# Projections, attentions, norms and gated sums of each block in one stage with a fixed order of steps

## The reference, cut to what matters

```
first block:  h = norm(x);  proj = h @ w_in -> xr, gr | dq, dk, dv | sq, sk, sv | gl
  o_lru  = gated linear recurrence(xr, gr)
  o_diff = 4 heads: softmax(norm(q0) norm(k0)^T + bias) - lam * softmax(norm(q1) norm(k1)^T + bias), causal, @ v
           then rms_norm over the head's 128 channels (sub-norm)
  o_swa  = 8 heads, 2 kv heads, window 128, with a sink logit per head
  merged = sum_n sigmoid(gl_n) * (o_n @ w_branch_n);   x += g * (merged @ w_out);  then a mixture of 32 experts
second block: h = norm(x);  proj = h @ w_in_2
  o_a = delta rule, both directions;  3 groups of 8 heads: window attention with dilation 1, 4, 16 (q, k normed)
  o_b = sum of the three groups, weighted by softmax of their log denominators
  mixed = sigmoid(gate_a) * (o_a @ w_dn_out) + sigmoid(gate_b) * (o_b @ w_attn_out);  x += mixed @ w_o;  then a gated FFN
```

## Time and profile before

| | us |
|---|---|
| median of 3 runs | 3631.92 (3628.58 to 3642.89) |
| the profiled execution | 3635.47 |
| its span, first to last instruction | 3633.5 |
| mean granted TensorE clock | 0.898 of full |

### The profile page before, as it was taken

How to read it: one execution, slowest core, us unless ns; L and a number is a source line. 1 busy time by engine, 2 the same in 40 slices (tenths; PEclk the granted TensorE clock), 3 DMA queues, 4 the chain that set the end, 5 groups by cost and what they waited for, 6 DMA issues and landing times. The chain is left out here.

```text
span 3633.5 us, 45934 instructions
## 1 busy us (share of the span) xinstructions
PE 3077.8 (85%) x18366; PEld 2419.9 (67%) x18366; DVE 2236.9 (62%) x2035; ACT 1594.3 (44%) x1712; POOL 250.9 (7%) x149
## 2 busy tenths in 40 slices
PE   7676669976899999999999909787868778979999
PEld 3554447764787788788878707686647665767777
DVE  6555643334798999999999744465545543336643
ACT  6523232221676777777777624222232331233322
POOL 0000000002011111111111000341000000000000
PEclk9886779995999999999999959898879777989999
DMA  7320102222899999999999741000202111223322
GB/s 310 99 71 18 47 1 93 93 97 111 308 370 370 367 373 376 372 373 372 376 370 379 272 149 63 14 4 26 75 13 70 47 35 47 93 59 93 93 81 81
DMA packets 207264, 604.81 MB, mean 166 GB/s; under 512 B 11426, under 2 KB 108706, under 8 KB 170500
## 3 DMA queue, kind: packets, MB, share of 16 engines
q1 hardware_dynamic: 197744, 568.52, 42.6%
q0 software_dynamic: 9216, 33.56, 2.5%
q10 hardware_dynamic: 148, 0.53, 0.0%
HBM read 581.57 MB, written 21.01 MB: 166 GB/s over the span
## 5 line engine op out<-in xcount | busy, mean ns | idle before, releaser
L1743 DVE TENSOR_TENSOR weight_ring_part<-weight_ring,weight_ring_part 128x2048 fp32r<-128x2048 f32 x384 | 860.5, 2284 | 103.0 <-ACT weight_ring_part L1684 102.9
L1684 ACT ACTIVATE weight_ring_part<-weight_ring 128x2048 fp32r<-128x2048 f32 x384 | 720.1, 1914 | 254.9 <-PE ps L192 132.6
L192 PE MATMUL ps<-weight_ring_part 128*128 128x512 f32 (+1 forms) x1328 | 527.6, 397 | 0.0
L287 DVE TENSOR_TENSOR weight_ring_part<-weight_ring,weight_ring_part 128x2048 fp32r<-128x2048 f32 x135 | 307.9, 2282 | 289.9 <-ACT weight_ring_part L284 288.2
L284 ACT ACTIVATE weight_ring_part<-weight_ring 128x2048 fp32r<-128x2048 f32 x135 | 256.8, 1903 | 369.8 <-PE ps L192 147.6
L190 PE MATMUL ps<-weight_ring_part,gathered_hi 128*128 128x512 f32 x1024 | 409.6, 400 | 1.8 <-DVE gathered_lo L1752 1.8
L192 PE MATMUL ps<-weight_ring_part,gathered_hi 128*128 128x512 f32 x1024 | 406.0, 396 | 0.0
L191 PE MATMUL ps<-weight_ring_part,gathered_lo 128*128 128x512 f32 x1024 | 405.9, 396 | 0.0
L190 PE MATMUL ps<-h1T_hi,weight_ring_part 128*128 128x512 f32 (+1 forms) x776 | 317.8, 409 | 54.3 <-PEq L339 29.3
L191 PE MATMUL ps<-h1T_hi,weight_ring_part 128*128 128x512 f32 (+1 forms) x776 | 307.9, 397 | 0.0
L192 PEld LDWEIGHTS ps<-weight_ring_part 128*128 128x128 f32 (+1 forms) x1328 | 253.3, 191 | 57.1 <-issue 0.8
(11 more groups left out here) (450 smaller groups left out, 4774.5 us busy)
## 6 DMA issues: line engine op xcount, KB each, us to landing
weight_ring<-in_w SPq DMA_DIRECT2D x190, 2048.0 KB, 9.1
weight_ring<-in_w_in SPq DMA_DIRECT2D x58, 1024.0 KB, 5.3
weight_ring<-in_w_ada SPq DMA_DIRECT2D x24, 1024.0 KB, 14.5
weight_ring<-in_w_ffn_up SPq DMA_DIRECT2D x44, 512.0 KB, 5.1
weight_ring<-in_w_ffn_down SPq DMA_DIRECT2D x11, 1024.0 KB, 4.9
chosen_rows<-y_rows SPq DMA_DIRECT2D x4, 2048.0 KB, 13.4
weight_ring<-in_w_branch SPq DMA_DIRECT2D x6, 1024.0 KB, 5.1
x_tok<-in_x SPq DMA_DIRECT2D x2, 2048.0 KB, 13.8
```

The costliest lines, as they stand in the source:

```text
L192: return nc.tensor.matmul(out, x[0], y[1], start=False, stop=stop)
L287: self.nc.vector.tensor_tensor(lo, full, hi, ALU.subtract).then_inc(self.split, 1)
L1684: nc.scalar.activation(hi_half(h), full_half(h), ACT.Copy).then_inc(w_rounded, 1)
L1743: nc.vector.tensor_tensor(lo_half(h), full_half(h), hi_half(h), ALU.subtract).then_inc(w_split, 1)
```

## The change: what it does

For each block, `project`, `attention`, the small stages and `merge_branches` are replaced by one stage, `stream`. A planner, `lay_out`, sets the order. It walks a list of **elements** (one element: 128 output channels; q, k, v, gate 8 k-steps, branch 4) and puts every other step at a place counted in k-steps; all engines then walk this one list, each doing its own part of every step.

The first block has 19 projection elements and 48 elements of gated sums, 440 k-steps; the second 36 and 32, 480 k-steps. The 24 attention units of each block start at k-steps 58 to 205 in the first and 58 to 306 in the second, 6, 5 or at least 8 k-steps apart. The gated sums' first element stands at k-step 152 and 288.

```diff
+def lay_out(elements, batches, units, gap, sources=(), subs=(), lse_from=None):
+    ...
+    for u in range(len(last_of) + 1):
+        put(last_of[u - 2] + 0.5 if u >= 2 else 0, "round", u)
+    for e, x in enumerate(elements):
+        put(ends[e], "out", e)
+        if x["kind"] == "v":
+            put(ends[e] + 2.5, "turn_v", e)
+    for b, batch in enumerate(batches):
+        done = ends[batch["elements"][-1]]
+        put(done + 2, "sums", b)
+        for j in range(len(batch["keys"])):
+            put(done + 5 + 2 * j, "spread", b, j)
+        spread_done[b] = done + 6 + 2 * len(batch["keys"])
+    for i, u in enumerate(units):
+        asked.append(max(asked[-1] + gap[i] if asked else 0, spread_done[u["batch"]]))
+    turned_at = [(min(asked[i + 2], asked[i] + 12) if i + 2 < N else asked[i] + 12) - 0.2 for i in range(N)]
+    for i in range(N):
+        put(asked[i], "scores", i)
+        put(min(asked[i + 1] + 0.3, asked[i] + 5) if i + 1 < N else asked[i] + 5, "norm", i)
+        put(turned_at[i], "turn", i)
+        put(turned_at[i] + 2, "weigh", i)
+        read_at.append(min(turned_at[i] + 5, turned_at[i + 1] + 0.1) if i + 1 < N else turned_at[i] + 5)
+        put(read_at[i], "read", i)
+    for h, i in enumerate(subs):
+        put(read_at[i] + 0.5, "sub_sums", h)
+        put(read_at[i] + 4, "sub_spread", h)
+    ...
+# PE: products of element e go to bank e % 2, which ACT alone empties
+if k0 == 0 and e >= 2:
+    copied(pe, e - 2)
+# PE: sums of squares, 4 matmuls of 128x2 per q or k element, instead of head_sum over 512 columns
+last = nc.tensor.matmul(ps[:, 2, at:at + 2], sq[:, slot_of_square(e), ...], head_sum[:, 0:P:HD], start=True, stop=True)
+# ACT: root of a batch of 4 elements (32 columns)
+nc.scalar.activation(root(b)[:, 0:m], ps[:, 2, 0:m], ACT.Sqrt, scale=1.0 / HD, bias=col("eps")).then_inc(rooted, 1)
+# DVE: reciprocal of 32 columns; for keys the factor is written out wide, PE transposes it, DVE multiplies
+nc.vector.reciprocal(factor(b)[:, 0:m], root(b)[:, 0:m])
+nc.vector.tensor_tensor(dst, dst, ps[:, 2, :], ALU.mult).then_inc(keys_scaled, 1)
+# DVE: the query's factor and the bias come with the scores, one instruction per segment
+for c, m, _, _, q_at, bias in u["scores"]:
+    last = nc.vector.scalar_tensor_tensor(s_row[:, c:c + m], scores[:, c:c + m], factor(u["batch"])[:, q_at:q_at + 1],
+                                          bias, ALU.mult, ALU.add)
+# ACT: gates by tanh (the table of the exponentials); branch copied out of PSUM
+nc.scalar.activation(merge["gate"][:, gate_at[e] % 2, :], bank, ACT.Tanh, scale=0.5)
+nc.scalar.activation(merge["branch"][:, branch_at[e] % 4, :], bank, ACT.Copy, scale=0.5)
-nc.vector.reciprocal(rinv, rinv)                      # 128x512, once per q or k element
-nc.tensor.matmul(ps[:, 4 + m % 2, :], head_sum, act_scratch[:, m % 2, :], start=True, stop=True)
+# second block: its input is stored once, since its room is used now, and loaded again in project_out
+sp.dma_start(x_mid.rearrange("(t p) d -> p t d", p=P), x_tok[:, :, :]).then_inc(x_stored, 16)
 sp.dma_start(w_ab, w_in2[:, 2048:2080].rearrange("(k p) n -> p k n", p=P)).then_inc(ab_loaded, 16)
 sp.dma_start(masks[:, :, :], a["joins"].rearrange("p (m i) -> p m i", i=HD)).then_inc(ab_loaded, 16)
```

More of the change, by code:

```diff
@@ L352, in build @@
         mix_at = len(ring.units)
-        for j in range(6):
-            ring.add_pair(wide(w_in, 512 * j), DK, 512, by_rows=(j == 4))
+        for j in range(2):
+            ring.add_pair(wide(w_in, 512 * j), DK, 512, by_rows=False)
+        for half in range(2):
+            for j in (4, 2, 3):
+                ring.add(wide(w_in, 512 * j)[:, :, 256 * half:256 * half + 256], DK, 256)
         w_kv = a["w_kv"].rearrange("(k p) n -> p k n", p=P)
@@ L382, in build @@
         for g in range(3):
-            for j in range(3):
-                ring.add_pair(wide(w_in2, 2080 + 1536 * j + 512 * g), DK, 512, by_rows=(j == 2))
+            for half in range(2):
+                for j in (2, 0, 1):
+                    ring.add(wide(w_in2, 2080 + 1536 * j + 512 * g)[:, :, 256 * half:256 * half + 256], DK, 256)
         for w, c0 in (("w_dn_out_2", 6688), ("w_attn_out_2", 7712)):
@@ new lines, in merge_elements @@
+        def merge_elements(elements, sources):
+            unit = max([e["unit"] for e in elements], default=-1) + 1
+            first = []
+            for n in range(sources):
+                first.append(len(elements))
+                for half in range(2):
+                    elements += [dict(kind="branch", unit=unit, part=m, ends=int(m == 3), source=n) for m in range(4)]
+                    elements += [dict(kind="gate", unit=unit + 1 + m // 2, part=m % 2, ends=m % 2, source=n, row=4 * half + m) for m in range(4)]
+                    unit += 3
+            return first
@@ L1138, in build @@
                 units.append(dict(
-                    scores=sc, seg=(4, 2 * P, w), bias=swa_bias[:, 4 * g:4 * g + 4, 2 * P - w:2 * P],
-                    sinks=col("swa_sinks", 4 * g, 4), turns=[2 * P * j + P * m for j in range(4) for m in range(w // P)],
-                    pv=pv, out=[(oT[:, 2, 2 * g:2 * g + 2, P * t:P * t + P], slice(0, P), slice(0, 2 * P))]))
-        attention(units, stats, s_buf, p_turned)
+                    scores=sc, seg=(4, 2 * P, w), batch=2 + g, at=32 + 4 * (len(units) - 16), needs=[15 + 2 * g, 16 + 2 * g], keys=6, v=5,
@@ new lines, in build @@
+        order = lay_out(elements, batches, units, [6] * 8 + [5] * 8 + [8] * 8, sources=firsts, subs=[4 * h + 3 for h in range(4)])
+        stream(hT, elements, batches, units, order, scratch4, factors, v_turn, stats, s_buf, p_turned,
+               sub=dict(rows=[oT[:, 1, h, :] for h in range(4)], units=[4 * h + 3 for h in range(4)], wide=side_room[:, 7680:8192],
+                        root=sub_root, gain=small[:, 40:41]),
+               merge=dict(sources=[(oT[:, n], his[n], oT_part[:, n]) for n in range(3)], out=chan(xn_flat, 0, DK), branch=half_x(x_tok[:, :, :], 0), room_free=[("values_ready", 16)],
+                          gate=work[:, 0:1024].rearrange("p (a b) -> p a b", a=2), gated=work[:, 1024:1536],
+                          after=[[("scores_read", 16)], [("subbed", 4), ("scores_ready", 24)], [("values_read", 24)]]))
@@ new lines, in build @@
+        for n in range(2, 12):
+            side[n].update(at=side[n - 1]["first"], free=side[n - 1]["first"] - 1)
+        firsts = merge_elements(elements, 2)
+        o_bT = o_g[:, 0]
+        half_x = lambda x, n: x.rearrange("p t d -> p (t d)")[:, 2048 * n:2048 * n + 2048].rearrange("p (c t) -> p c t", c=BC)
+        hi_b = arena_part[:, 0:2048].rearrange("p (c t) -> p c t", c=BC)
+        order = lay_out(elements, batches, units, [6] * 8 + [5] * 8 + [8] * 8, sources=firsts, lse_from=(0, 4, 8, 13, 24))
@@ new lines, in build @@
+        stream(h1T, elements, batches, units, order, squares2, factors2, v_turn2, stats2, s_buf2, p_turned2,
+               merge=dict(sources=[(dn_out[:, :, :], half_x(x_part[:, :, :], 0), dn_out_part[:, :, :]), (o_bT, hi_b, o_g_part[:, 0])],
+                          out=chan(xn_flat, 0, DK), branch=half_x(x_tok[:, :, :], 1), room_free=[], gate=arena[:, 6656:7680].rearrange("p (a b) -> p a b", a=2), gated=arena[:, 7680:8192], after=[[], [("weights_read", 13)]]),
+               side=side, lse_of=dict(sums=stats2[:, 1, :], lse=lse, turned=lse_t, most=lse_m, selector=selector, out=o_g))
@@ L2573, in build @@
+        project_out((chan(xn_flat, 0, DK), h1T_hi, as_chunks(xn_part[:, :, :])), None, load_x=x_mid)
         att.close()
```

773 lines of the change are left out of this document (588 added, 185 removed).

## The result

The changed kernel takes 3574.5 us (median of 4 runs, 3573.8 to 3577.8); the kernel before took 3633.5 in the same job. The ratio is 0.984, with an interval of 0.982 to 0.986. It is faster by 59 us, and I had forecast 176: 3456 us, with a range up to 3550. The profiled execution has a span of 3575.7 us.

A forecast was written before the change was run, and what follows sets the result against it. PE's work of 872 us was the floor, the order of steps the added bound: plus waits 46 + 38, clock 16 and store 7, 979 us for 1154.8, giving 3456 us; own range 3405 to 3510, stated range 3385 to 3550.

The forecast's parts named there:

- the clock: New attention stretches, some 190 and 325 us long: granted clock 0.93, costing 8 + 8 us beyond the waits.
- The rival of the falling clock: Waits keep the clock at 1.2 GHz through two thirds of the attention stretches: 3722 us, chance 0.04.
- The waits' sum: PE's waits in both new stages, for attention units, norms and group weights: 46 + 38 us, 84 us.
- the window units of the first block: Window attention, 8 units: 11.4 us of DVE and ACT per unit against 10 of PE, 11 us of waits.
- the sub-norms: First block's four sub-norms: 2.5 us of PE wait for each round trip between engines.
- Both signs of a wrong forecast: A first-attention unit under 6.9 or over 9 us, or a clock under 0.85 in the attention stretches.
- PE's work: Matmul time the new stages cannot go below: 406 and 466 us, 872 in all, with 3 us per stage start.
- my price of a k-step: Three matmuls on PE: 0.730 us in the first block, 0.713 in the second, including the short wait at weight units' ends.
- The store: Storing x, 2 MB, ahead of two small loads delays the second block's first stage: 7 us, between 0 and 13.8.
- The lockstep rival: DVE's and ACT's work adds up: 9.5 us per unit for 32 units, 3 more for 16 others; 3568 us, chance 0.16.
- PE as the bound: Rival: PE bounds nearly everywhere, with waits of 15 us, clock loss 5 and store 5; 3374 us, chance 0.15.
- A stall at the table switches: Rival: switching ACT's tables stalls it longer than the load, 18 us more on the path; 3474 us, chance 0.05.

The follow-up runs named there:

- run 2: Changed kernel with the turn and weighing of the turned probabilities four k-steps later for units 16 and up: 3528.0 us, ratio 0.972.
- run 9: Changed kernel with 12 spare matmuls of 512 columns ahead of PE's wait for the turned probabilities, units 16 and up: 3571.4 us, ratio 0.982.
- run 4: Changed kernel with the sub-norm's square as its own ACT step, 4.5 k-steps ahead of its sums: 3559.6 us, ratio 0.981.
- run 7: Changed kernel with the second block's sums of squares issued four per element, two k-steps after its product, not 16 in a row: 3566.3 us, ratio 0.981.
- run 1: Changed kernel with the key_gain tile taking 64 bytes a partition instead of 4, moving later buffers by 60 bytes: 3573.6 us, ratio 0.984.
- run 8: Changed kernel with later turns, 32-column sums of squares, earlier sub-norm square, group weights in four steps, x stored behind the small loads: 3496.2 us, ratio 0.961.
- run 3: Changed kernel with the second block's sums-of-squares matmuls 32 columns wide instead of two: 3564.0 us, ratio 0.982.

## Why the prediction was wrong

**The step that failed** is the clock: "I take 0.93, and half of the loss falls into waits: 8 + 8 us". The clock's cost is 36.0 + 43.7 us, 64 more than that, out of 107 us by which the two stages miss the forecast (503.0 + 576.4 against 460 + 512). I took the mean busy share and read a mean clock from it. But rows 2 and 3 show stages that wait everywhere or nowhere; the first block's new stage waits 2 to 7 us at a time in dense work, and 3.4 to 10 us at half speed go with each such wait. Runs 2 and 9 show it: where the waits went, the clock's cost went with them, and where PE was kept busy through the same six waits the clock stayed up. In the second block a quarter of the cost is of this kind. The rest came where I had priced no clock at all: some 21 us at the rows of sums, without a wait, and 12 at the weights of the groups, behind a wait of 5.6 us. The Trainium skill (TensorE: Matmul & The Clock Gate, "HAM oscillation — how this bites in real kernels") tells of a kernel that pays for such falls again and again, one behind each wait, with half the time at the low clock as the price; the low stretches between units 18 and 23 were 23.9 us in sum, half is 12, and run 9 gained 9. The rival of the falling clock had the mechanism with too large an extent (two thirds of the stretch at 1.2 GHz, 3722 us).

**The waits' sum was right, their places were not.** I had 84 us and 90 are there. For the window units of the first block I had 11 us, at 11.4 us a unit; the last five took 14.9 each, and 22 us of wait stand before the weighings there (six, from 461.2 on). The reason isn't the sum of DVE's and ACT's work, as I argued, but one copy's place behind the exponentials, a copy out and a rounding; four k-steps later for the turn are 10.1 us a unit (run 2). For the sub-norms I had 4 x 2.5 us; they took 18.0 in three waits, because PE's sums were issued right behind the square (run 4). In the second block the 16 units of the first group took 7.4 us each, inside the 6.9 to 9 that I named; in the first block 9.5, over it, with the sub-norms inside. Both signs of a wrong forecast thus came in the first block: a unit over 9 us, and a clock under 0.85 (0.84).

**The rows of narrow matmuls** weren't in the forecast as a cost of the clock. Run 7, which spread them out, took 16 us off the second block's clock cost, and the whole was 8 us faster, since new waits came with it. What in such a row lowers the clock, its width or its length, is open.

**PE's work.** Products, other matmuls at full clock and the unit ends are 310.0 + 75.0 + 13 = 398 and 338.2 + 130.6 + 14 = 483 us, against 403 and 463 without the stages' start: 5 less, and 20 more. Of the 20, some 7 are the products' distance, 0.232 us in this stage where the rows behind my price of a k-step had 0.227 (1440 products). Some 8 are the sums of squares of the second and third group's queries, whose stationary is read with a step of four tokens: at full clock a record takes 0.23 us there and 0.11 with tokens in a row, and I had one price for both. In run 7 the four matmuls of one element, first with the step and then without (timeline of PE):

```profile
2666.86 1.80 PE L1152 MATMUL ps<-const,weight_ring 128*128 128x2 f32 x8
2690.44 0.95 PE L1152 MATMUL ps<-const,weight_ring 128*128 128x2 f32 x8
```

What is left of each stage, 14 us, is pauses too short for the accounting and the stage's two ends, where I had 3: 22 us in sum. With 64 for the clock, 6 for the waits and 15 for PE's work that is the 107. The long reciprocals went as said: DVE is at 200.8 us where it was at 254.3; what that was worth by itself no run shows.

**The store** was about right: a first product 6.1 us later, 4.5 of them shown to be the store's, against 7.

**Outside the stages** 17.6 us came up, of which the store is 7 at most. By run 1 the placement of the buffers moves the rate of the products in stages whose code is the same; why is open.

**The rivals.** The lockstep rival gave 3568, near what was measured, but not for its reason: it wanted 9.5 us for each of 32 units, and outside the sub-norms and the starts of batches the first 16 units of either block follow each other after 5.2 to 8.8, but for one 11.1. The first block's mean of 9.5 is that number by chance: it comes from the sub-norms and the starts of batches. The kernel's time came from elsewhere. PE as the bound (3374) asked for waits of 15 us and is far. A stall at the table switches doesn't show: the root at 427.9 us starts 1.29 us after its load does. By the rule of the Trainium skill named in the forecast (ScalarE: Activation LUTs, "What ACT_TABLE_LOAD costs") the drains would be 19 us more; ACT's table loads take 1.28 us here as before, and no run shows the drain.

What stays open: in the second block run 8 still pays 31 us to the clock, nearly half of it at or behind rows of sums; and how the places at which it falls come to differ between executions of the same code (65 or 51 us of low stretches in the same piece).

## What to carry to other kernels

Where an order of steps mixes attention with products, price a wait of PE of 2 us and more at its length plus the stretch at half speed behind it, here nearly as much again, and look in each engine's list at what stands ahead of the one short copy for which PE waits. A few k-steps between an instruction's step on one engine and its use on another were worth 61 us here (runs 2 and 4), as much as the whole rewriting, at no cost in work. Look as well at rows of very narrow matmuls: here the clock fell at them without any wait. When nothing can be moved, spare matmuls inside the wait hold the clock, but where there is no wait they are added time.

## What the runs showed of the hardware

- In the first block of the changed kernel the granted clock was at 0.5 for 3.4 to 10 us, once 20.5, during or behind each of fourteen waits of PE of 1.6 to 7.5 us; four waits of 1.0 to 1.6 us in the second block had no low stretch. With matmuls inside six of these waits it stayed at 1.0 through them (run 9, 444 to 540 us).
- The clock fell to 0.5 for 6.8 us, once 10.2, at six rows of 16 matmuls of two columns (4.4 to 6.7 us long) without a wait. With 32 columns it held at the first two rows (run 3), but with two columns it also held at the first in run 2, and with 32 it fell behind the first in run 8. With four at a time between k-steps the low stretches were mostly 3.4 us instead of 6.8 (run 7).
- Records of matmuls with 8 rows and 512 columns started 0.853 us apart at low clock (the changed kernel) and 0.43 apart at full clock (run 8).
- A record of a matmul of two columns took 0.11 us start to start when the 128 columns of its stationary lay in a row and 0.23 when they were read with a step of four (both at full clock, run 7).
- The median distance of products of the same shape was 0.227 to 0.234 us by stage, and moved by up to 0.006 when the buffers behind one 4-byte tile were moved by 60 bytes (run 1).
